# Squares of the new residual: added in tile pairs on VectorE before TensorE sums them, against summed by TensorE alone

## The reference

```python
def rmsnorm(x, g):
    y = xf * lax.rsqrt(jnp.mean(xf * xf, axis=-1, keepdims=True) + RMS_EPS)
    return (y * g).astype(x.dtype)

def residual_update(x, h_m, attn, w_out, g_post_mix, g_pre_ffn, w_ffn_in, w_ffn_out, g_post_ffn):
    x = x + rmsnorm(jnp.concatenate([h_m, attn], axis=-1) @ w_out, g_post_mix)
    h = rmsnorm(x, g_pre_ffn)
    gate, up = jnp.split(h @ w_ffn_in, 2, axis=-1)
    return x + rmsnorm((jax.nn.silu(gate) * up) @ w_ffn_out, g_post_ffn)
```

## Time and profile before

| | |
|---|---|
| median of three executions | 3164.11 us (3161.0 to 3166.08) |
| the profiled execution | 3163.28 us, span 3161.5 us |
| PE busy | 2995.7 us, 95% of the span |
| PEld busy | 2776.2 us, 88% |
| DVE busy | 1283.1 us, 41% |
| ACT busy | 586.4 us, 19% |
| POOL busy | 1003.9 us, 32% |
| matmuls of `new_x_squares`, line 580 | 72, in 144 records, near 774 to 805, 1574 to 1609 and 2334 to 2365 us |

### The profile page before, as it was taken

One profiled execution on the slowest core, in us unless ns is written; L12 is line 12 of the kernel. 1 busy time (PEld: TensorE's weight loads), 2 busy tenths in 40 slices (PEclk: granted clock), 3 DMA queues, 4 the chain that ended last, 5 costly groups with the idle time before them and its releaser, 6 DMA issues.

```text
span 3161.5 us, 41563 instructions
## 1 busy us (share of the span) xinstructions
PE 2995.7 (95%) x17424; PEld 2776.2 (88%) x17424; DVE 1283.1 (41%) x1547; ACT 586.4 (19%) x967; POOL 1003.9 (32%) x474
## 2 busy tenths in 40 slices
PE   6999989989999999999989998999899999999998
PEld 6989866678999999999879987666889999999997
DVE  7433344544532323333482334355463323233235
ACT  3212233432200000000231223244230000000002
POOL 3222232124234333333222223223223333333440
PEclk8999979999999999999999999799999999999999
DMA  5221110021111111111122111000211111111111
GB/s 162 35 38 36 29 36 1 1 82 47 34 40 46 51 42 46 46 46 40 31 82 50 29 29 35 29 1 7 82 40 46 48 41 46 46 46 40 41 51 56
DMA packets 210327, 137.04 MB, mean 43 GB/s; under 512 B 49256, under 2 KB 201384, under 8 KB 209712
## 3 DMA queue, kind: packets, MB, share of 16 engines
q1 hardware_dynamic: 195904, 108.78, 13.1%
q10 hardware_dynamic: 14320, 26.83, 2.3%
HBM read 119.64 MB, written 15.94 MB: 43 GB/s over the span
## 4 chain that ended last, share of the span: by engine, by line
PE 82%; issue 6%; DVE 5%; POOLq 2%; ACT 2%; DVEq 1%; POOL 1%; PEld 1%; ACTq 1%; PEldq 0%; SPq 0%
PE acc L558 17%; PE acc L562 16%; PE acc L561 16%; PE acc L1027 5%; PE acc L1031 5%; PE acc L1030 5%; PE acc L933 3%; PE acc L537 3%; PE acc L538 3%; PE acc L539 3%; DVE residual L1563 1%; PE acc L805 1%; PE acc L696 1%; PE acc L712 1%; DVE branch L1561 1%
## 5 line engine op out<-in xcount | busy, mean ns | idle before, releaser
L558 PE MATMUL acc<-act_hi,slab_hi 128*128 128x352 f32 x2640 | 865.3, 328 | 35.9 <-ACT residual L1236 12.6
L562 PE MATMUL acc<-act_lo,slab_hi 128*128 128x352 f32 x2640 | 852.3, 323 | 0.0
L561 PE MATMUL acc<-act_hi,slab_lo 128*128 128x352 f32 x2640 | 850.4, 322 | 0.0
L433 POOL TENSOR_TENSOR slab_hi<-slab_raw,ones 128x1024 fp32r<-128x1024 f32 x144 | 275.6, 1914 | 1189.5 <-PE acc L558 665.5
L558 PEld LDWEIGHTS acc<-act_hi,slab_hi 128*128 128x128 f32 x2640 | 497.8, 189 | 49.5 <-issue 46.6
L561 PEld LDWEIGHTS acc<-act_hi,slab_lo 128*128 128x128 f32 x2640 | 499.7, 189 | 0.0
L562 PEld LDWEIGHTS acc<-act_lo,slab_hi 128*128 128x128 f32 x2640 | 499.1, 189 | 0.0
L435 POOL TENSOR_TENSOR slab_lo<-slab_raw,slab_hi 128x1024 fp32r<-128x1024 f32 x144 | 360.2, 2501 | 21.5 <-issue 0.9
L1958 DVE TENSOR_TENSOR branch<-acc,branch 128x1056 f32<-128x1056 f32 x160 | 201.3, 1258 | 393.4 <-PE acc L1031 393.4
L1948 DVE TENSOR_TENSOR work<-acc,work 128x1056 f32<-128x1056 f32 x44 | 55.2, 1255 | 590.7 <-PE acc L562 590.7
L433 POOL TENSOR_TENSOR small_hi<-slab_raw,ones 128x1024 fp32r<-128x1024 f32 x50 | 97.1, 1942 | 515.4 <-PEq L1034 369.0
(11 more groups left out here) (377 smaller groups left out, 4931.9 us busy)
## 6 DMA issues: line engine op xcount, KB each, us to landing
slab_raw<-in_w_ffn_in SPq DMA_DIRECT2D x88, 512.0 KB, 3.7
slab_raw<-in_w_ffn_out SPq DMA_DIRECT2D x44, 512.0 KB, 3.2
slab_raw<-in_w_in SPq DMA_DIRECT2D x40, 512.0 KB, 5.0
x_spill<-residual ACTq DMA_DIRECT2D x2, 4224.0 KB, 13.1
residual<-x_spill ACTq DMA_DIRECT2D x2, 4224.0 KB, 13.0
slab_raw<-in_w_out SPq DMA_DIRECT2D x16, 512.0 KB, 3.7
branch<-in_x_prompt ACTq DMA_DIRECT2D x4, 1024.0 KB, 8.9
out_y_prompt<-out_rows SPq DMA_DIRECT2D x8, 512.0 KB, 2.7
```

The lines of the kernel that those rows point to most:

```text
L433: pool.tensor_tensor(hi, raw, ONES[:, 0:1].broadcast_to([P, SLAB]), ALU.mult)
L558: mm = pe.matmul(out, wh, HH[:, x], start=k == 0, stop=False)
L561: pe.matmul(out, wl, HH[:, x], start=False, stop=False)
L562: mm = pe.matmul(out, wh, HL[:, x], start=False, stop=k == KT - 1)
```

## The change

VectorE gets a new step, `fold_squares(z, n, i)`: when the squares of pairs 2i and 2i+1 of group n are there, it adds the second pair onto the first in place (one 704-column fp32 addition, line 1568 of the changed kernel) and signals `x_sq_folded`. PE's `new_x_squares` waits for these two signals in place of the four of ACT, and runs four matmuls with the ones, not eight. That is two additions more on DVE and four matmuls less on PE for each of 3 groups in 3 passages: 18 additions, 36 matmuls.

In DVE's order both additions of group 0 and the first of groups 1 and 2 stand among the `new_x` steps; the second one of groups 1 and 2 stands inside `normed` of the group before, behind its first two scaled copies.

```diff
             def new_x_squares(z, n):
 
-                for j in range(KT // 2):
-                    pe.wait_ge(x_sq, ((z - 1) * 3 + n) * 4 + j + 1)
-                    if j == 0:
+                for i in range(2):
+                    pe.wait_ge(x_sq_folded, ((z - 1) * 3 + n) * 2 + i + 1)
+                    if i == 0:
                         pe.wait_ge(pre_rs, (z - 1) * 3 + n)
-                    for k in (2 * j, 2 * j + 1):
-                        mm = pe.matmul(bank(7, TG), ONES[:, :], part(SQX, k, n), start=k == 0, stop=k == KT - 1)
+                    for k in (4 * i, 4 * i + 1):
+                        mm = pe.matmul(bank(7, TG), ONES[:, :], part(SQX, k, n), start=k == 0, stop=k == 5)
                 mm.then_inc(pre_ms, 1)
...
-            def normed(l, z, n):
+            def fold_squares(z, n, i):
+
+                dve.wait_ge(x_sq, ((z - 1) * 3 + n) * 4 + 2 * i + 2)
+                dve.tensor_tensor(pair(SQX, 2 * i, n), pair(SQX, 2 * i, n), pair(SQX, 2 * i + 1, n), ALU.add).then_inc(x_sq_folded, 1)
+
+            def normed(l, z, n, fold=None):
...
                     e.then_inc(h_scaled, 1)
+                    if j == 0 and fold is not None:
+                        fold_squares(z, fold, 1)
                     if j:
                         lo(j - 1)
...
-                for n in range(2):
-                    for j in range(4):
-                        new_x(l, y, n, j)
-                normed(l, z, 0)
+                for j in range(4):
+                    new_x(l, y, 0, j)
+                fold_squares(z, 0, 0)
+                new_x(l, y, 1, 0)
+                fold_squares(z, 0, 1)
+                for j in range(1, 4):
+                    new_x(l, y, 1, j)
+                fold_squares(z, 1, 0)
+                normed(l, z, 0, fold=1)
                 for j in range(4):
                     new_x(l, y, 2, j)
-                normed(l, z, 1)
+                fold_squares(z, 2, 0)
+                normed(l, z, 1, fold=2)
                 normed(l, z, 2)
...
                 if l < LAYERS - 1:
+                    fold_squares(z, 0, 0)
+                    fold_squares(z, 0, 1)
                     for j in range(4):
                         new_x(l, y, 1, j)
+                    fold_squares(z, 1, 0)
                     for m in range(4, KT):
                         add_sum(2, m)
-                    normed(l + 1, z, 0)
+                    normed(l + 1, z, 0, fold=1)
                     for j in range(4):
                         new_x(l, y, 2, j)
-                    normed(l + 1, z, 1)
+                    fold_squares(z, 2, 0)
+                    normed(l + 1, z, 1, fold=2)
                     normed(l + 1, z, 2)
```

More of the change, by code:

```diff
@@ L251, in encoder_step @@
         post_ms, post_rs, pre_ms, pre_rs = sem("post_ms"), sem("post_rs"), sem("pre_ms"), sem("pre_rs")
-        x_new, x_sq = sem("x_new"), sem("x_new_square")
+        x_new, x_sq, x_sq_folded = sem("x_new"), sem("x_new_square"), sem("x_square_folded")
         h_scaled, h_hi, h_part = sem("h_scaled"), sem("h_hi"), sem("h_part")
```

## The result

The changed kernel took 3174.08 us (median of 10 runs, 3166.89 to 3180.42), the kernel before 3164.6 us in the same series (10 runs, 3158.61 to 3172.76). The ratio is 1.0031, 95% interval 1.0020 to 1.0042: slower by 9.8 us. The profiled execution took 3171.52 us, its span is 3169.7 us, 8.2 more than before.

A forecast was written before the change was run, and what follows sets the result against it. The chain is 82% PE, but DVE's order was taken to set side_by_side(1)'s start between the layers and, after the change, in middle passages. 2 x 2.2 + 3.2 + 1.2 = 8.8 us slower, 3172.5 us, range 3165 to 3179.

The forecast's parts named there:

- Which engine sets the end: Start of side_by_side(1): DVE's low part of group 1 releases it in middle passages, +2.2 us each; between the layers +3.2 us.
- side_by_side(1) released by the low part of DVE: Sign expected in the profile after: PE's side_by_side(1) waits for DVE's low part, starting 2 to 3 us later in middle passages.
- rival B: Middle passages: group 2's sums ready when PE comes, two groups give 2.37 us each, -9.5 us, 3154; chance 0.06.
- Price of an addition, 0.8 us: DVE's 704-column addition of squares priced like line 1563, 0.8 us; lower bound 0.49, upper bound 2.62 beside POOL.
- Rival A: VectorE's lead is enough: an addition costs 0.49 us, +0.6 a middle passage, +2.0 between the layers, 3166.5; chance 0.14.
- Lead of 1.9 us and five additions in a middle passage: DVE leads by 1.9 us; five additions move group 1's first low part 4.0 later, to 806.7, +2.2 us a passage.
- The sums of group 0 cost nothing: Middle passage: these sums end at 780.5, not 779.2, but PE must wait until 786.4 anyway, so no cost.
- The clock, 0.4 us a passage: Half clock after PE's new idle stretch, mostly hidden in slow matmuls and DVE wait: 0.4 us a passage, +1.2 in all.
- the rule that the prediction cites: Trainium skill, matmul and clock gate: warns against idle gaps above about 3 us between bursts of matmuls; speaks against this change.
- I take the loss as unchanged, with 1 us either way: Between the layers: POOL starts about 1.4 us sooner, but DVE's loss beside its four operations stays 5.7 us.
- by more than 1 us: Sign of being wrong: POOL's shift changes DVE's loss between the layers by more than 1 us.
- Rival C: The clock decides: low level lasts beyond 806.75 by a second slow stretch, 1.75 us more each passage, 3177; chance 0.16.

## Why the prediction was right, step by step

Forecast: 3172.5 us, slower. Measured: 3174.08; 9.8 us by the ratio, where 8.8 were worked out.

- *Which engine sets the end.* Right in the main. The low part of group 1 comes 30.2 us behind new_x in a middle passage both in the changed kernel and with additions alone, 4.0 later than before, and with the clock held up it is what releases side_by_side(1). Without filler PE's own slow sums come 0.6 us after it, so the sign "side_by_side(1) released by the low part of DVE" held between the layers only. Taking the matmuls out alone gives at most 8 us, where rival B wanted 9.5, and in the passages +0.4. That additions alone (1.0033) match the whole change (1.0031) proves less than it seems, since the clock fell at different places in the two.
- *Price of an addition, 0.8 us.* Right: 0.88 long, the next starts 0.80 later. It is the form of line 1563 in the earlier trace rows. Rival A's 0.49 is out. Doubling all additions moved DVE's low part by 4.0 us in a middle passage, five times this price, and by 4.5 between the layers, where 4.6 were expected; the total of 12.4 against 12.6 is closer than its parts.
- *Lead of 1.9 us and five additions in a middle passage.* Right: the low part comes 30.23 us behind new_x, exactly the 806.7 - 776.47 that was worked out. With the clock held up by filler the passage is 46.5 us, the forecast +2.2.
- *The sums of group 0 cost nothing.* Right in the end, though by another course. PE waited 2.82 us between their two halves, and the clock fell then too, from the sums into the 24 projection matmuls (5.83 us, not 4.3). Its next wait was 0.55 us, not 2.46, and the branch sums came 1.15 later than before, not 0.8. All of it lay under the later wait of 4.12 us for DVE.
- *The clock, 0.4 us a passage.* Mis-sized in the middle: 1.1 us there, 0 between the layers, 2.2 in all where 1.2 was forecast. I took it that most of the slow stretch would fall on four slow matmuls inside the wait for DVE. The four matmuls at the lower level took 5.06 us, and with them PE started 0.6 us behind DVE's low part, in the slow stretch still. The trace before also agrees less well than I wrote with the rule that the prediction cites: of its two slow stretches only the one behind 3.65 us of idle time fits it. The pause ahead of 1558.8 is 2.04 us, and in the changed kernel the clock fell behind one of 2.82 us too, while in the kernel before it did not behind one of 2.46 us.
- *Between the layers, "I take the loss as unchanged, with 1 us either way".* This step failed: the loss beside GpSimd went from 5.7 to 7.4 us, so the passage grew by 5.0 and not by 3.6. It is one of the prediction's own signs of being wrong ("by more than 1 us"), and it came true. I had seen that POOL would start 1.4 us sooner (it was 1.3), but counted its four operations and not what they meet. Before, the second of them met four additions out of PSUM, which it does not disturb; now it met scaled copies. The additions-only kernel separates the two causes: there POOL starts at its old place, 7.0 us behind new_x, with the same additions on DVE, and the loss is 6.0. So the addition itself brings 0.3 us of it, and the earlier start, which comes from the matmuls taken out, 1.4. Holding POOL back in the changed kernel brought the loss to 5.9 and the passage down by 1.3.
- *Together.* Middle +3.3 and +3.4 (2.6 expected with the clock), between +5.0 (3.6): passages +11.7 us, where 8.8 were forecast. The whole kernel grew by about 2 us less than its passages, within what the rest of it varies by. So the closeness of 3172.5 to 3174.08 is partly luck.
- *Rival C.* A second slow stretch did follow: the low level lasted until about 806.8, past DVE's low part. All of the clock together cost 1.1 us in a middle passage, where the forecast had 0.4 and C 1.75 more.

## What to carry to other kernels

Before moving work from a busy engine to an idle one, measure the lead of the receiving engine at the place where the giving one next waits for it: here it was 1.9 us, enough for one addition of 0.8, not for five, though DVE was 41% busy over all. Work that is taken out just ahead of a wait can bring less than it was worth, by a clock that falls in the longer pause (half the matmuls: 0.6 us a middle passage, 1.8 with filler), or even lengthen a passage, by another engine that starts sooner and meets different instructions (+1.65 us between the layers). Where two engines contend, list which instructions overlap, not only how long. And when a control run is meant to leave out a cause, look in its trace whether it did: the additions-only kernel kept PE's work and still had slow stretches.

## What the runs showed of the hardware

Two things I had not expected.

Useless matmuls can shorten a passage. PE's pause of 4.95 us was followed by six records in 3.88 us; with 4.41 us of filler in the pause they took 2.05, and the passage was 1.2 us shorter. In the changed kernel 3.55 us of filler gave back 1.1 us a middle passage. The time of the whole kernel did not show it in either case (1.0007 with filler against 0.9984 without; 1.0025 against 1.0031).

What GpSimd costs VectorE depends on the operands. Four 352-column additions with one input in PSUM took 1.80 and 1.81 us at two places beside GpSimd and 1.80 without it, while a 704-column addition of two SBUF inputs took 0.88 alone and up to 3.03, a pair of scaled copies 1.07 alone and 4.80.
